# Modulation rows split over two stages: shift and scale by column quarters on turned tokens, gates and second norm during the first block's projections

## The chip, the cores and the metric

The kernel runs on one core of a Trainium2 chip. Its engines run in parallel and meet through semaphores: TensorE (PE, matrix products and transposes into PSUM; its weight loads are listed as PEld), VectorE (DVE), ScalarE (ACT), GpSimd (POOL) and SyncE (SP, which here only starts transfers). The metric is the time of one execution on the device in microseconds (us), smaller is better. The inputs are laid out on the host; all arithmetic is on the chip.

## What is computed

Two blocks of a transformer-like network over 1024 tokens of width 1024, all in 32-bit floats. What matters here is how the first block starts and where the vector `mod` goes:

```python
cond = jax.nn.silu(c)                              # (1, 1024)
mod = cond @ ada_w[l] + ada_b[l]                   # (1, 6144)
sh_m, sc_m, gt_m, sh_f, sc_f, gt_f = [t[:, None, :] for t in jnp.split(mod, N_MOD, axis=-1)]
h = rms_norm(x, norm_mix_g[l]) * (1.0 + sc_m) + sh_m
proj = jnp.einsum('bsd,de->bse', h, w_in[l])
...
x = x + gt_m * (merged @ w_out[l])
h = rms_norm(x, norm_mlp_g[l]) * (1.0 + sc_f) + sh_f
x = x + gt_f * (jnp.square(jax.nn.relu(h @ mlp_w1[l])) @ mlp_w2[l])
```

Only the first third of `mod` (sh_m, sc_m) is needed for the first projections. The other four vectors are needed when the mixers have been merged, far later.

## The kernel before

The program is a row of stages. Each is a `Stage`: it owns buffers and semaphores, and at its end all engines meet at a barrier, so no stage starts before the last instruction and the last awaited store of the one before. The stages that matter are "mod" (`mod_norm_stage`), then "scans", "diff_gemm" (`diff_gemm_stage`), "diff", and all the others behind them. Within a stage the order of each engine is the order in which it is written; there is no scheduler.

**The stage "mod".** SP loads the tokens `x` (8 tiles of 128 tokens, 4 MB) and then, through a ring of four 2 MB slots, the weights `ada_w` in 12 chunks of 512 columns (`NCH` is 12); a slot is loaded again when DVE has released it. ScalarE makes silu of the condition (`cact`, the 1024 values as 8 columns of 128) and the sums of squares of the token tiles (L216). For each chunk c:

- TensorE multiplies the first four of the eight k blocks of the chunk (L278): the stationary matrix is `cwide`, the condition repeated over 128 columns, so that the result stands on all 128 partitions;
- DVE does the other four k blocks as multiply-adds over 128x512 into `acc` (L231, `partial`), and TensorE sums `acc` over the partitions with a matrix of ones into the same PSUM bank (L280);
- DVE copies the chunk to `mod` (L240, `take`).

When chunks 0 to 3 (shift and scale) are there, DVE scales the gain once (L263), and then normalizes the token tiles, two passes each (`norm`: L245 and L246), two buffers `h` in turn. The table `NORMED` puts them behind chunks 4 to 9. TensorE turns each tile (8 transposes, L286, which in the program stand behind the products of the next chunk), and ScalarE moves it into `hT`, the turned tokens that all projections read (L221). POOL stores the rows of the chunks 4 to 11 (gates and second norm) to the array `mod_rows` in HBM (L204), and the stage waits for these stores. "scans" starts with its own loads (L2797) and splits `hT` and weights into high and low parts for three-pass products (L155, L156, L157).

**The stage "diff_gemm"** makes 24 result tiles n of 128x512, each by 8 k blocks of three passes on TensorE (L155 to L157), evicted by ScalarE (L1871) and stored by SP. Its weights come in five pieces (1 MB each from the second on), cast on ScalarE (L1862, L1866), and DVE subtracts to get the low part (`low_w`: L1881, L1885). TensorE waits for a piece at the tiles 8, 12, 16 and 20 (`LAST`). DVE has nothing else to do there, and POOL nothing at all. Its columns 0 to 511 of `oN` are not in use.

**Elsewhere**: the routers of the expert stages (L3430) already make products of 32 columns of weights at four column places of the array; they serve the prediction as a measure.

Of the kernel before, what the change touches and what calls it, by code (L numbers as in the profile page):

```python
# [6 lines left out]
F32 = mybir.dt.float32  # L7
# [6 lines left out]
P = 128  # L14
S = 1024
D = 1024
# [143 lines left out]
def mod_norm_stage(nc, m):  # L160


    with Stage(nc, "mod") as st:
        NCH, K2 = 6 * D // HALF, KD // 2
        first = m["ring"].take(NCH)
        x = m["oN"]
        ccol, cact = st.sb("ccol", [P, KD]), st.sb("cact", [P, KD])
        cwide, ones = st.sb("cwide", [P, K2, P]), st.sb("ones", [P, P])
        bias, mod = st.sb("bias", [P, NCH, HALF]), st.sb("mod", [P, NCH, HALF])
        acc = st.sb("acc", [P, 2, HALF])  # L170
        h, g = st.sb("h", [P, 2, D]), st.sb("gain", [P, D])
        ss, rs = st.sb("ss", [P, NT]), st.sb("rs", [P, NT])
        out, TP = st.ps("out", [P, 2, HALF]), st.ps("tp", [P, 2, KD, P])
        (loaded, zeroed, bias_in, act_done, wide, summed_up, summed, added, stored, squared, mean_in, root, gain_ready,
         scaled, h_ready, turned_up, tp_free, stepped) = (
            st.sem(x_) for x_ in ("loaded", "zeroed", "bias_in", "act_done", "wide", "summed_up", "summed", "added",
                                  "stored", "squared", "mean_in", "root", "gain_ready", "scaled", "h_ready", "turned_up",
                                  "tp_free", "stepped"))
        x_in = [st.sem(f"x_in{t}") for t in range(NT)]
        block = st.block()  # L180
        NORMED = {4: (0,), 5: (1, 2), 6: (3,), 7: (4, 5), 8: (6,), 9: (7,)}
        flat = mod[:, :, :].rearrange("p c n -> p (c n)")
        shift, scale = flat[:, 0:D], flat[:, D:2 * D]

        def slot(c):
            return m["ring"].slot(first + c, KD, HALF)

# [7 lines left out]
        def _(pool):  # L195
# [5 lines left out]
            pool.dma_start(bias[0:1, :, :].rearrange("p c n -> p (c n)"), m["ada_b"][0:1, :]).then_inc(bias_in, 16)  # L201
            for c in range(4, NCH, 2):
                pool.wait_ge(added, c + 2)
                pool.dma_start(m["mod"][0:1, c * HALF:(c + 2) * HALF], flat[0:1, c * HALF:(c + 2) * HALF])\  # L204
                    .then_inc(stored, 16)
            pool.wait_ge(stored, 16 * (NCH - 4) // 2)

        @block.scalar
        def _(act):
# [3699 lines left out]
```

## Time and profile before

| what | value |
|---|---|
| median of 3 runs | 4243.39 us (4241.23 to 4247.34) |
| the profiled execution, its own time | 4248.85 us |
| its span, first to last instruction | 4247.0 us |
| TensorE busy in the span | 3730.8 us (88%) |
| VectorE, ScalarE, GpSimd busy | 2463.2 (58%), 1626.5 (38%), 354.2 us (8%) |
| granted TensorE clock, mean | 0.939 of full |
| first transfer of the stage "scans" | at 104.27 us |
| "diff_gemm" | from 772.25 to 913.14 us |

The span starts with the first instruction. Because the stages meet at barriers, what a stage takes is the distance between the first transfers of two neighbours, and what one stage gets shorter, all later ones start earlier.

### The profile page before, as it was taken

What the parts mean: (1) busy time and instruction counts of PE and PEld (TensorE: products, weight loads), DVE (VectorE), ACT (ScalarE), POOL (GpSimd) and SP (SyncE); (2) the same over time, 40 slices, a digit from 0 to 9 for tenths busy, and PEclk for the clock granted to TensorE, in tenths of its full rate; (3) what the DMA queues carried; (4) which work ended last, traced back from release to release, by engine and by line L of the source; (5) the groups of instructions that cost most, each with busy time, mean ns of one, the idle gap of its engine ahead of it and who ended that gap; (6) DMA issues with size and microseconds to landing.
All of it is one profiled execution on the core that took longest, in us unless ns stands there. A gap on an engine that the chain in (4) does not pass through costs nothing. (4 is left out here: it accounts for less than half of the span.)

```text
span 4247.0 us, 58233 instructions
## 1 busy us (share of the span) xinstructions
PE 3730.8 (88%) x23192; PEld 3037.4 (72%) x23192; DVE 2463.2 (58%) x3913; ACT 1626.5 (38%) x2293; POOL 354.2 (8%) x205
## 2 busy tenths in 40 slices
PE   6988999989898999999798998499886998984996
PEld 2666778767777888888598776377686776773774
DVE  6257764129765655656332663777664666636785
ACT  2223342138531000002212763366534666623765
POOL 0001112000000000000000000144100000000441
PEclk9989999989999999999899999699898999996998
DMA  7201122331342111112222415399724103042997
GB/s 284 73 25 50 55 70 86 103 129 40 129 155 80 40 59 40 59 40 80 78 75 70 132 44 189 134 371 368 248 77 131 36 7 127 24 144 100 372 368 273
DMA packets 192273, 527.06 MB, mean 124 GB/s; under 512 B 27137, under 2 KB 126241, under 8 KB 174001
## 3 DMA queue, kind: packets, MB, share of 16 engines
q1 hardware_dynamic: 172576, 463.01, 30.0%
q0 software_dynamic: 16352, 58.84, 4.6%
q8 instruction: 156, 2.56, 0.2%
q10 hardware_dynamic: 3120, 2.10, 0.2%
q14 instruction: 69, 0.56, 0.0%
HBM read 432.52 MB, written 91.37 MB: 123 GB/s over the span
## 5 line engine op out<-in xcount | busy, mean ns | idle before, releaser
L2462 ACT ACTIVATE mlp_relu<-mlp_z 128x512 f32<-128x512 f32 x64 | 38.3, 598 | 616.0 <-PE mlp_z L157 616.0
L155 PE MATMUL scans_G<-ring_r 128*128 128x512 f32 x544 | 221.7, 408 | 32.3 <-ACT scans_stg L3009 18.3
L3584 DVE TENSOR_TENSOR ring_r<-ring,oN_r 128x4096 fp32r<-128x4096 f32 x48 | 212.4, 4426 | 64.1 <-ACT oN_r L3512 63.5
L3584 DVE TENSOR_TENSOR ring_r<-ring,hT_r 128x4096 fp32r<-128x4096 f32 x48 | 212.3, 4423 | 61.5 <-ACT hT_r L3512 61.4
L3512 ACT ACTIVATE oN_r<-ring 128x4096 fp32r<-128x4096 f32 x48 | 174.0, 3630 | 82.6 <-DMA ring<-in_w_all 68.4
L155 PE MATMUL mlp_z<-oN_r,mlp_w_high_r 128*128 128x512 f32 x512 | 200.2, 391 | 5.6 <-DVE ring_r L2503 5.6
L3512 ACT ACTIVATE hT_r<-ring 128x4096 fp32r<-128x4096 f32 x48 | 174.0, 3629 | 76.5 <-DMA ring<-in_w_all 76.5
L156 PE MATMUL mlp_z<-hT_r,mlp_w_high_r 128*128 128x512 f32 x512 | 199.9, 390 | 0.0
L157 PE MATMUL mlp_z<-oN_r,ring_r 128*128 128x512 f32 x512 | 199.9, 390 | 0.0
L155 PE MATMUL mlp_y_ps<-mlp_w_high_r,ring_r 128*128 128x512 f32 x512 | 199.6, 390 | 0.0
L157 PE MATMUL mlp_y_ps<-mlp_w_high_r,ring_r 128*128 128x512 f32 x512 | 199.2, 389 | 0.0
L156 PE MATMUL mlp_y_ps<-ring_r 128*128 128x512 f32 x512 | 199.2, 389 | 0.0
L3398 POOL TENSOR_TENSOR moe_taker<-moe_zero 128x1 f32<-128x1 f32 x63 | 160.5, 2548 | 412.1 <-ACT moe_y L3574 399.5
L156 PE MATMUL scans_G<-hT_r,ring_r 128*128 128x512 f32 x480 | 191.9, 400 | 0.0
L157 PE MATMUL scans_G<-ring_r 128*128 128x512 f32 x480 | 191.2, 398 | 0.0
L2513 DVE TENSOR_TENSOR mlp_relu<-mlp_relu 128x512 f32<-128x512 f32 x64 | 44.2, 691 | 182.0 <-ACT mlp_relu L2462 173.1
L155 PEld LDWEIGHTS scans_G<-ring_r 128*128 128x128 f32 x544 | 104.9, 193 | 59.1 <-issue 14.7
L2524 DVE TENSOR_TENSOR mlp_y<-mlp_y_ps,mlp_gt 128x512 f32<-128x512 f32 x128 | 88.2, 689 | 99.0 <-PE mlp_y_ps L157 96.6
L155 PE MATMUL even_gemm_acc<-even_gemm_w_high,ring_r 128*128 128x384 f32 x384 | 133.7, 348 | 5.0 <-DVE ring_r L673 5.0
L157 PE MATMUL even_gemm_acc<-even_gemm_w_high,hT_r 128*128 128x384 f32 x384 | 129.7, 338 | 0.0
L2860 POOL TENSOR_TENSOR ring_r<-ring,ring_r 128x2048 fp32r<-128x2048 f32 (+1 forms) x16 | 73.7, 4607 | 567.8 <-ACT ring_r L3014 567.8
L155 PEld LDWEIGHTS mlp_z<-oN_r,mlp_w_high_r 128*128 128x128 f32 x512 | 96.6, 189 | 26.1 <-issue 6.0
(666 smaller groups left out, 10196.4 us busy)
## 6 DMA issues: line engine op xcount, KB each, us to landing
ring<-in_w_all SPq DMA_DIRECT2D x118, 2048.0 KB, 10.7
ring<-in_w_mlp SPq DMA_DIRECT2D x16, 2048.0 KB, 8.4
ring<-in_w_all SPq DMA_DIRECT2D x12, 1024.0 KB, 6.2
branch_gates<-scans_stg SPq DMA_DIRECT2D x48, 256.0 KB, 2.0
merge_raw<-branch_gates SPq DMA_DIRECT2D x16, 768.0 KB, 5.1
ring<-in_w_even SPq DMA_DIRECT2D x4, 1536.0 KB, 6.7
qk_turned<-even_gemm_y SPq DMA_DIRECT2D x48, 128.0 KB, 1.9
ring<-qk_turned SPq DMA_DIRECT2D x6, 1024.0 KB, 5.0
```

Source lines behind the costliest of these rows:

```text
L155: pe.matmul(out, lh, rh, start=start, stop=False)
L156: pe.matmul(out, lh, rl, start=False, stop=False)
L157: return pe.matmul(out, ll, rh, start=False, stop=stop)
L2462: act.activation(r[:, n % 2, :], Z[:, n % 4, :], ACT.Relu).then_inc(z_free, 1)
L2513: step(dve.tensor_tensor(r[:, n % 2, :], r[:, n % 2, :], r[:, n % 2, :], ALU.mult))
L2524: dve.tensor_tensor(y[:, n % 2, :], Y[:, n % 4, :], gt[:, cols], ALU.mult).then_inc(y_free, 1)
L2860: pool.tensor_tensor(low, raw, high.bitcast(F32), ALU.subtract).then_inc(w_split, 1)
L3398: pool.tensor_tensor(taker[:, n:n + 1], zero[:], zero[:], ALU.add)
L3512: act.activation(w_high[n % RING], buf[:, (first + n) % RING, :], ACT.Copy).then_inc(w_cast, 1)
L3584: dve.tensor_tensor(buf_r[:, b, :], buf[:, b, :], w_high[n % RING].bitcast(F32), ALU.subtract)\
```

## The change

- "mod" takes only the chunks 0 to 3. The ring's limit goes from 12 to 4, the later `skip` from 8 to 16.
- For a chunk, TensorE now does all eight k blocks, as products with 32 columns of weights (`ccols`), k block k at the column quarter k % 4 of the array, so on 32 partitions each (`Q`). DVE adds the bias (`quart`), and one product with `sel` (ones at the partitions 0, 32, 64 and 96) sums the quarters on all partitions. `partial` is gone.
- The tokens are only scaled by their inverse root before they are turned, on ScalarE (`h`, in turn with the move into `hT`). Shift and (1 + scale) * gain are turned to columns (8 transposes each, into `Q` and `out`), and applied at the end to the eight 128x1024 blocks of `hT`: three on ScalarE, five on DVE.
- "diff_gemm" gets the chunks 4 to 11: POOL fills `SUMS` (in `oN`) with zeros and the bias, and loads 16 halves of chunks, 1 MB each, into three places (second halves of weight slots); DVE adds each with four multiply-adds of 128x512 behind each `low_w` (`add_part`). Ahead of tile 21, TensorE sums them over the partitions (8 products with 32 columns of ones), ScalarE moves the sums, and POOL stores the rows in `mod_rows`.

```diff
@@ -161,29 +161,32 @@
...
     with Stage(nc, "mod") as st:
-        NCH, K2 = 6 * D // HALF, KD // 2
+        NCH = 2 * D // HALF
...
-        ccol, cact = st.sb("ccol", [P, KD]), st.sb("cact", [P, KD])
-        cwide, ones = st.sb("cwide", [P, K2, P]), st.sb("ones", [P, P])
+        ccol, cact = st.sb("ccol", [P, KD]), m["cact"]
+        ccols, sel = st.sb("ccols", [P, KD, 32]), st.sb("sel", [P, P])
...
-        acc = st.sb("acc", [P, 2, HALF])
+        quart = st.sb("quart", [P, 2, HALF])
...
+        cols = st.sb("cols", [P, 2, KD])
+        Q, out, TP = st.ps("quarters", [P, 2, HALF]), st.ps("out", [P, 2, HALF]), st.ps("tp", [P, 2, KD, P])
...
-        NORMED = {4: (0,), 5: (1, 2), 6: (3,), 7: (4, 5), 8: (6,), 9: (7,)}
...
+        ON_ACT = (5, 6, 7)
...
-            pool.dma_start(bias[0:1, :, :].rearrange("p c n -> p (c n)"), m["ada_b"][0:1, :]).then_inc(bias_in, 16)
-            for c in range(4, NCH, 2):
-                pool.wait_ge(added, c + 2)
-                pool.dma_start(m["mod"][0:1, c * HALF:(c + 2) * HALF], flat[0:1, c * HALF:(c + 2) * HALF])\
-                    .then_inc(stored, 16)
-            pool.wait_ge(stored, 16 * (NCH - 4) // 2)
+            pool.dma_start(bias[0:1, :, :].rearrange("p c n -> p (c n)"), m["ada_b"][0:1, 0:2 * D]).then_inc(bias_in, 16)
+            pool.memset(sel[:], 0.0).then_inc(zeroed, 1)
+            pool.wait_ge(zeroed, 2)
+            for j in range(4):
+                pool.memset(sel[32 * j:32 * j + 1, :], 1.0).then_inc(sel_in, 1)
...
@@ -216,75 +218,100 @@
                 act.activation(h[:, 0, :], x[:, t, :], ACT.Square, accum_out=ss[:, t:t + 1]).then_inc(squared, 1)
             act.wait_ge(mean_in, 1)
             act.activation(rs[:], ss[:], ACT.Sqrt).then_inc(root, 1)
-            for t in range(NT):
-                act.wait_ge(turned_up, t + 1)
-                act.activation(m["hT"][:, :, t * P:(t + 1) * P], TP[:, t % 2, :, :], ACT.Copy).then_inc(tp_free, 1)
+            act.wait_ge(squared, NT)
+            act.wait_ge(inverse, 1)
+            for t in range(NT + 1):
+                if t < NT:
+                    if t >= 2:
+                        act.wait_ge(turned_up, t - 1)
+                    act.activation(h[:, t % 2, :], x[:, t, :], ACT.Copy, scale=rs[:, t:t + 1]).then_inc(h_ready, 1)
+                if t >= 1:
+                    act.wait_ge(turned_up, t)
+                    act.activation(m["hT"][:, :, (t - 1) * P:t * P], TP[:, (t - 1) % 2, :, :], ACT.Copy).then_inc(tp_free, 1)
+            act.wait_ge(tp_free, NT)
+            act.wait_ge(cols_in, 1)
+            for k in ON_ACT:
+                act.activation(m["hT"][:, k, :], m["hT"][:, k, :], ACT.Identity, bias=cols[:, 1, k:k + 1],
+                               scale=cols[:, 0, k:k + 1])
...
         @block.vector
...
-            def partial(c):
-                w, a = slot(c), acc[:, c % 2, :]
-                m["ring"].wait(dve, first + c)
-                for k in range(K2, KD):
-                    ins = dve.scalar_tensor_tensor(a, w[:, k, :], cact[:, k:k + 1], bias[:, c, :] if k == K2 else a,
-                                                   ALU.mult, ALU.add)
-                    if k < KD - 1:
-                        step(ins)
-                ins.then_inc(summed_up, 1)
...
             def take(c):
                 dve.wait_ge(summed, c + 1)
-                m["ring"].release(dve)
-                dve.tensor_copy(mod[:, c, :], out[:, c % 2, :]).then_inc(added, 1)
-
-            def norm(t):
-                if t >= 2:
-                    dve.wait_ge(turned_up, t - 1)
-                step(dve.scalar_tensor_tensor(h[:, t % 2, :], x[:, t, :], rs[:, t:t + 1], g[:], ALU.mult, ALU.mult))
-                dve.tensor_tensor(h[:, t % 2, :], h[:, t % 2, :], shift, ALU.add).then_inc(h_ready, 1)
+                if c < NCH // 2:
+                    dve.tensor_copy(mod[:, c, :], out[:, c % 2, :]).then_inc(taken, 1)
+                else:
+                    n = (c - NCH // 2) * HALF
+                    dve.scalar_tensor_tensor(mod[:, c, :], out[:, c % 2, :], 1.0, g[:, n:n + HALF], ALU.add, ALU.mult)\
+                       .then_inc(taken, 1)
...
             dve.wait_ge(act_done, 1)
-            step(dve.memset(ones[:], 1.0))
-            dve.tensor_copy(cwide[:], cact[:, 0:K2].unsqueeze(2).to_broadcast([P, K2, P])).then_inc(wide, 1)
+            dve.tensor_copy(ccols[:, :, :], cact[:].unsqueeze(2).to_broadcast([P, KD, 32])).then_inc(wide, 1)
...
             for c in range(NCH):
-                partial(c)
+                dve.wait_ge(waved, c + 1)
+                m["ring"].release(dve)
+                if c >= 2:
+                    dve.wait_ge(summed, c - 1)
+                dve.tensor_tensor(quart[:, c % 2, :], Q[:, c % 2, :], bias[:, c, :], ALU.add).then_inc(quartered, 1)
                 if c >= 1:
                     take(c - 1)
-                if c == 3:
-                    dve.wait_ge(squared, NT)
-                    dve.tensor_scalar(ss[:], ss[:], 1.0 / D, EPS, ALU.mult, ALU.add).then_inc(mean_in, 1)
-                    dve.wait_ge(root, 1)
-                    step(dve.reciprocal(rs[:], rs[:]))
-                if c == 4:
-                    dve.wait_ge(added, 4)
-                    step(dve.scalar_tensor_tensor(g[:], scale, 1.0, g[:], ALU.add, ALU.mult))
-                for t in NORMED.get(c, ()):
-                    norm(t)
             take(NCH - 1)
+            dve.wait_ge(shift_turned, 1)
+            dve.tensor_copy(cols[:, 1, :].unsqueeze(2), blocks(Q)[:, :, 0:1])
+            dve.wait_ge(gain_turned, 1)
+            dve.tensor_copy(cols[:, 0, :].unsqueeze(2), blocks(out)[:, :, 0:1]).then_inc(cols_in, 1)
+            dve.wait_ge(cols_in, 1)
+            dve.wait_ge(tp_free, NT)
+            for k in range(KD):
+                if k not in ON_ACT:
+                    dve.tensor_scalar(m["hT"][:, k, :], m["hT"][:, k, :], cols[:, 0, k:k + 1], cols[:, 1, k:k + 1],
+                                      ALU.mult, ALU.add)
...
         @block.tensor
         def _(pe):
+            def turn(t):
+                pe.wait_ge(h_ready, t + 1)
+                if t >= 2:
+                    pe.wait_ge(tp_free, t - 1)
+                for k in range(KD):
+                    ins = pe.transpose(TP[:, t % 2, k, :], h[:, t % 2, k * P:(k + 1) * P], m["ident"][:])
+                ins.then_inc(turned_up, 1)
...
             pe.wait_ge(wide, 1)
             pe.wait_ge(m["ident_in"], 16)
+            pe.wait_ge(sel_in, 4)
             for c in range(NCH):
                 w = slot(c)
                 m["ring"].wait(pe, first + c)
                 if c >= 2:
-                    pe.wait_ge(added, c - 1)
-                for k in range(K2):
-                    pe.matmul(out[:, c % 2, :], cwide[:, k, :], w[:, k, :], start=k == 0, stop=False)
-                pe.wait_ge(summed_up, c + 1)
-                pe.matmul(out[:, c % 2, :], ones[:], acc[:, c % 2, :], start=False, stop=True).then_inc(summed, 1)
...
+                    pe.wait_ge(quartered, c - 1)
+                for k in range(KD):
+                    j = slice(32 * (k % 4), 32 * (k % 4) + 32)
+                    ins = pe.matmul(Q[j, c % 2, :], ccols[:, k, :], w[:, k, :], start=k < 4, stop=k >= 4)
+                ins.then_inc(waved, 1)
+                turn(2 * c)
+                if c + 1 < NCH:
+                    turn(2 * c + 1)
+                pe.wait_ge(quartered, c + 1)
+                if c >= 2:
+                    pe.wait_ge(taken, c - 1)
+                pe.matmul(out[:, c % 2, :], sel[:], quart[:, c % 2, :], start=True, stop=True).then_inc(summed, 1)
+            pe.wait_ge(taken, 2)
+            for k in range(KD):
+                ins = pe.transpose(blocks(Q)[:, k, :], flat[:, k * P:(k + 1) * P], m["ident"][:])
+            ins.then_inc(shift_turned, 1)
+            turn(NT - 1)
+            pe.wait_ge(taken, NCH)
+            for k in range(KD):
+                ins = pe.transpose(blocks(out)[:, k, :], flat[:, D + k * P:D + (k + 1) * P], m["ident"][:])
+            ins.then_inc(gain_turned, 1)
...
@@ -1789,7 +1816,16 @@
...
+        rows = st.ps("rows", [P, 2, HALF])
...
+        PARTS, SUMS = 16, m["oN"][:, :, 0:HALF]
+        parts = [t_[:, b, SLOT // 2:SLOT].rearrange("p (k n) -> p k n", n=HALF) for t_, b in ((buf, 1), (more, 0), (more, 1))]
@@ -1831,9 +1867,35 @@
...
+        @block.gpsimd
+        def _(pool):
+            pool.memset(ONE[:], 1.0).then_inc(ones_in, 1)
+            pool.memset(SUMS, 0.0).then_inc(zeroed, 1)
+            pool.wait_ge(zeroed, 1)
+            pool.dma_start(SUMS[0:1, :, :], m["ada_b"][0:1, 2 * D:6 * D].rearrange("o (c n) -> o c n", n=HALF))\
+                .then_inc(bias_in, 16)
+            for i in range(PARTS):
+                if i >= len(parts):
+                    pool.wait_ge(part_added, i - len(parts) + 1)
+                c, half = divmod(i, 2)
+                pool.dma_start(parts[i % len(parts)], m["w_all"][4 + c, :, half * SLOT // 2:(half + 1) * SLOT // 2]
+                               .rearrange("p (k n) -> p k n", n=HALF)).then_inc(part_in[i % len(parts)], 16)
+            pool.wait_ge(rows_out, 2)
+            for c in range(PARTS // 2):
+                pool.dma_start(m["mod"][0:1, 2 * D + c * HALF:2 * D + (c + 1) * HALF],
+                               parts[0][32 * (c % 4):32 * (c % 4) + 1, c // 4, :]).then_inc(rows_stored, 16)
+            pool.wait_ge(rows_stored, 16 * PARTS // 2)
...
         @block.tensor
         def _(pe):
             for n in range(N):
+                if n == N - 3:
+                    pe.wait_ge(ones_in, 1)
+                    pe.wait_ge(sums_done, 1)
+                    for c in range(PARTS // 2):
+                        ins = pe.matmul(rows[32 * (c % 4):32 * (c % 4) + 32, c // 4, :], ONE[:], SUMS[:, c, :],
+                                        start=True, stop=True)
+                    ins.then_inc(rows_done, 1)
@@ -1869,6 +1931,10 @@
...
                 act.activation(x[:, n % KEEP, :], A[:, n % 4, :], ACT.Copy).then_inc(x_in, 1)
+                if n == N - 3:
+                    act.wait_ge(rows_done, 1)
+                    for j in range(2):
+                        act.activation(parts[0][:, j, :], rows[:, j, :], ACT.Copy).then_inc(rows_out, 1)
...
+            def add_part(i):
+                c, half = divmod(i, 2)
+                dve.wait_ge(part_in[i % len(parts)], 16 * (i // len(parts) + 1))
+                for k in range(4):
+                    kk = 4 * half + k
+                    ins = dve.scalar_tensor_tensor(SUMS[:, c, :], parts[i % len(parts)][:, k, :], m["cact"][:, kk:kk + 1],
+                                                   SUMS[:, c, :], ALU.mult, ALU.add)
+                    if k < 3:
+                        step(ins)
+                ins.then_inc(part_added, 1)
+                dve.wait_ge(part_added, i + 1)
+
+            step = Steps(dve, stepped)
+            dve.wait_ge(bias_in, 16)
             for s_ in range(1, NS):
                 low_w(s_)
+                for i in range(4 * s_ - 4, 4 * s_):
+                    add_part(i)
+            dve.nop().then_inc(sums_done, 1)
@@ -3709,12 +3792,13 @@
...
-        m["ring"].limit = 12
...
+        m["ring"].limit = 4
...
-        m["ring"].skip(8)
+        m["ring"].skip(16)
```

How TensorE's order changes in the stage "mod". Before, from the end of chunk 4 on (`mod_tp` are the turned tokens; the pattern goes on to chunk 11):

```order
L280 MATMUL mod_out<-mod_acc,mod_ones 128x512
L278 MATMUL mod_out<-ring,mod_cwide 128x512 x4
L280 MATMUL mod_out<-mod_acc,mod_ones 128x512
L286 MATMUL mod_tp<-identity,mod_h 128x128 x8
L278 MATMUL mod_out<-ring,mod_cwide 128x512 x4
L280 MATMUL mod_out<-mod_acc,mod_ones 128x512
L286 MATMUL mod_tp<-identity,mod_h 128x128 x16
L278 MATMUL mod_out<-ring,mod_cwide 128x512 x4
L280 MATMUL mod_out<-mod_acc,mod_ones 128x512
```

The same engine and stage now, the last two chunks and the end of the stage:

```order
L297 MATMUL mod_quarters<-ring,mod_ccols 32x512 x8
L284 MATMUL mod_tp<-identity,mod_h 128x128 x16
L305 MATMUL mod_out<-mod_quart,mod_sel 128x512
L297 MATMUL mod_quarters<-ring,mod_ccols 32x512 x8
L284 MATMUL mod_tp<-identity,mod_h 128x128 x8
L305 MATMUL mod_out<-mod_quart,mod_sel 128x512
L308 MATMUL mod_quarters<-identity,mod_mod 128x128 x8
L284 MATMUL mod_tp<-identity,mod_h 128x128 x8
L313 MATMUL mod_out<-identity,mod_mod 128x128 x8
```

The tiles are now turned from the first chunk on, and nothing of chunks 4 to 11 is left. DVE in "diff_gemm", from its second piece of weights on, now (before, these splits, then L1881, followed each other with nothing between):

```order
L1947 TENSOR_TENSOR ring_r<-ring,diff_gemm_w_high 128x2048
L1958 SCALAR_TENSOR_TENSOR oN<-ring,cact,oN 128x512 x4
L1958 SCALAR_TENSOR_TENSOR oN<-diff_gemm_more,cact,oN 128x512 x8
L1958 SCALAR_TENSOR_TENSOR oN<-ring,cact,oN 128x512 x4
L1947 TENSOR_TENSOR diff_gemm_more_r<-diff_gemm_more,diff_gemm_w_high 128x2048
L1958 SCALAR_TENSOR_TENSOR oN<-diff_gemm_more,cact,oN 128x512 x8
L1958 SCALAR_TENSOR_TENSOR oN<-ring,cact,oN 128x512 x4
L1958 SCALAR_TENSOR_TENSOR oN<-diff_gemm_more,cact,oN 128x512 x4
L1947 TENSOR_TENSOR diff_gemm_more_r<-diff_gemm_more,diff_gemm_w_high 128x2048
```

So 16 multiply-adds stand behind each split of weights, 64 in all, and the last split has 16 multiply-adds of the third group ahead of it.

## Rows read from the trace of the kernel before

**Rows 1.** Busy time of each engine in the two changed stages.
```profile
core 0: us, PE busy (x) PEld busy (x) DVE busy (x) ACT busy (x) POOL busy (x), PEclk, DMA share, GB/s
0.00:104.27 104.27, 66.22 (x184) 31.81 (x184) 64.48 (x81) 20.15 (x28) 9.75 (x13) 0.96 0.71 288
772.25:913.14 140.89, 132.99 (x576) 109.57 (x576) 13.66 (x6) 25.28 (x30) 0.00 (x0) 0.97 0.22 75
```

**Rows 2.** Groups by line up to 105 us: mean ns, then idle time before.
```profile
L278 PE MATMUL mod_out<-ring,mod_cwide 128*128 128x512 f32 x96 | 45.8, 622 | 22.1 <-DMA ring<-in_w_all 22.1
L231 DVE SCALAR_TENSOR_TENSOR mod_acc<-ring,mod_cact,mod_acc 128x512 f32<-128x512 f32 x36 | 27.1, 752 | 1.3
L221 ACT ACTIVATE hT<-mod_tp 128x1024 f32<-128x1024 f32 x8 | 8.1, 1023 | 48.0 <-PE mod_tp L286 48.0
```

**Rows 3.** Timeline of the end of the stage "mod", and first transfer of "scans".
```profile
99.97 0.69 DVE L240 COPY mod_mod<-mod_out 128x512 f32<-128x512 f32 x1 [2.28 <-PE mod_out L280]
100.96 0.48 POOL L204 DMA_DIRECT2D mod_rows<-mod_mod  x1 [6.11 <-DVE mod_mod L240]
104.27 0.40 SPq L2797 DMA_DIRECT2D scans_c<-in_w_all  x1
```

**Rows 4.** Timeline: ScalarE's table load; DVE at the first and fourth slot.
```profile
20.20 1.28 ACT L218 ACT_TABLE_LOAD   x1
21.85 0.75 DVE L231 SCALAR_TENSOR_TENSOR mod_acc<-ring,mod_cact,mod_bias 128x512 f32<-128x512 f32 x1 [10.68 <-DMA ring<-in_w_all]
36.45 0.75 DVE L231 SCALAR_TENSOR_TENSOR mod_acc<-ring,mod_cact,mod_bias 128x512 f32<-128x512 f32 x1 [1.18 <-DMA ring<-in_w_all]
```

**Rows 5.** Timeline of TensorE in "mod"; each product is two passes (x8 are four).
```profile
21.88 6.09 PE L278 MATMUL mod_out<-ring,mod_cwide 128*128 128x512 f32 x8 [21.88 <-DMA ring<-in_w_all]
28.67 3.60 PE L278 MATMUL mod_out<-ring,mod_cwide 128*128 128x512 f32 x8
53.01 1.04 PE L286 MATMUL mod_tp<-identity,mod_h 128*128 128x128 f32 x8
60.58 1.80 PE L280 MATMUL mod_out<-mod_acc,mod_ones 128*128 128x512 f32 x2 [3.10 <-DVE mod_acc L231]
```

**Rows 6.** Timeline of weight loads at the routers of the two expert stages.
```profile
2647.61 0.20 PEld L3430 LDWEIGHTS moe_u_ps<-hT,moe_wr_wide 128*32 128x32 f32 x4 [0.66 <-issue]
2648.46 0.20 PEld L3430 LDWEIGHTS moe_u_ps<-hT,moe_wr_wide 128*32 128x32 f32 x4 [0.66 <-issue]
...
3829.54 0.12 PEld L3430 LDWEIGHTS moe_u_ps<-hT,moe_wr_wide 128*32 128x32 f32 x4 [0.34 <-issue]
3829.97 0.12 PEld L3430 LDWEIGHTS moe_u_ps<-hT,moe_wr_wide 128*32 128x32 f32 x4 [0.31 <-issue]
```

**Rows 7.** Groups by form: 128x1024 in SBUF with a scalar for each partition.
```profile
L3194 DVE TENSOR_SCALAR scans_T<-scans_T,scans_om 128x1024 f32<-128x1024 f32 x4 | 3.0, 751 | 0.1
L3077 ACT ACTIVATE scans_KQ<-scans_KQ,scans_lb 128x1024 f32<-128x1024 f32 x4 | 4.4, 1141 | 0.0
```

**Rows 8.** Timeline of DVE in "diff_gemm", second and last piece of weights.
```profile
792.35 2.29 DVE L1881 TENSOR_TENSOR ring_r<-ring,diff_gemm_w_high 128x2048 fp32r<-128x2048 f32 x1 [13.64 <-ACT diff_gemm_w_high L1862]
868.51 2.29 DVE L1881 TENSOR_TENSOR ring_r<-ring,diff_gemm_w_high 128x2048 fp32r<-128x2048 f32 x1 [19.47 <-ACT diff_gemm_w_high L1862]
```

**Rows 9.** Timeline of ScalarE and SP: the tiles 20 and 23, the next stage.
```profile
893.27 0.60 ACT L1871 ACTIVATE diff_gemm_x<-diff_gemm_acc 128x512 f32<-128x512 f32 x1 [4.84 <-PE diff_gemm_acc L157]
909.59 0.60 ACT L1871 ACTIVATE diff_gemm_x<-diff_gemm_acc 128x512 f32<-128x512 f32 x1 [4.84 <-PE diff_gemm_acc L157]
913.14 0.34 SPq L1934 DMA_DIRECT2D diff_lp<-in_diff_lambda  x1
```

**Rows 10.** Issues of transfers: KB each, us from issue to landing.
```profile
diff_gemm_more<-in_w_diff SPq DMA_DIRECT2D x2, 1024.0 KB, 9.7
x_rows<-out_x POOLq DMA_DIRECT2D x8, 512.0 KB, 2.9
qk_turned<-diff_gemm_x SPq DMA_DIRECT2D x16, 256.0 KB, 2.0
mod_rows<-mod_mod POOLq DMA_DIRECT2D x4, 4.0 KB, 3.7
```

More of the change, by code:

```diff
@@ L171, in mod_norm_stage @@
         h, g = st.sb("h", [P, 2, D]), st.sb("gain", [P, D])
         ss, rs = st.sb("ss", [P, NT]), st.sb("rs", [P, NT])
[L173 to L178, printed above, removed]
+        cols = st.sb("cols", [P, 2, KD])
@@ new lines, in mod_norm_stage @@
+        Q, out, TP = st.ps("quarters", [P, 2, HALF]), st.ps("out", [P, 2, HALF]), st.ps("tp", [P, 2, KD, P])
+        (loaded, zeroed, sel_in, bias_in, act_done, wide, waved, quartered, summed, taken, squared, mean_in, root, inverse,
+         h_ready, turned_up, tp_free, shift_turned, gain_turned, cols_in, stepped) = (
+            st.sem(x_) for x_ in ("loaded", "zeroed", "sel_in", "bias_in", "act_done", "wide", "waved", "quartered", "summed",
+                                  "taken", "squared", "mean_in", "root", "inverse", "h_ready", "turned_up", "tp_free",
+                                  "shift_turned", "gain_turned", "cols_in", "stepped"))
@@ L179, in mod_norm_stage, with blocks @@
         x_in = [st.sem(f"x_in{t}") for t in range(NT)]
         block = st.block()
-        NORMED = {4: (0,), 5: (1, 2), 6: (3,), 7: (4, 5), 8: (6,), 9: (7,)}
         flat = mod[:, :, :].rearrange("p c n -> p (c n)")
-        shift, scale = flat[:, 0:D], flat[:, D:2 * D]
+        ON_ACT = (5, 6, 7)
         def slot(c):
             return m["ring"].slot(first + c, KD, HALF)
+        def blocks(ps):
+            return ps[:, :, :].rearrange("p a n -> p (a n)").rearrange("p (k n) -> p k n", n=P)
@@ L251, in _ @@
+            dve.wait_ge(act_done, 1)
+            dve.tensor_copy(ccols[:, :, :], cact[:].unsqueeze(2).to_broadcast([P, KD, 32])).then_inc(wide, 1)
+            dve.wait_ge(squared, NT)
+            dve.tensor_scalar(ss[:], ss[:], 1.0 / D, EPS, ALU.mult, ALU.add).then_inc(mean_in, 1)
+            dve.wait_ge(root, 1)
+            dve.reciprocal(rs[:], rs[:]).then_inc(inverse, 1)
             dve.wait_ge(bias_in, 16)
             for c in range(NCH):
-                partial(c)
+                dve.wait_ge(waved, c + 1)
[3 more added lines that the diff above has]
+                dve.tensor_tensor(quart[:, c % 2, :], Q[:, c % 2, :], bias[:, c, :], ALU.add).then_inc(quartered, 1)
@@ L275, in _ @@
                 if c >= 2:
-                    pe.wait_ge(added, c - 1)
-                for k in range(K2):
-                    pe.matmul(out[:, c % 2, :], cwide[:, k, :], w[:, k, :], start=k == 0, stop=False)
-                pe.wait_ge(summed_up, c + 1)
-                pe.matmul(out[:, c % 2, :], ones[:], acc[:, c % 2, :], start=False, stop=True).then_inc(summed, 1)
-                for t in NORMED.get(c - 1, ()):
-                    pe.wait_ge(h_ready, t + 1)
-                    if t >= 2:
-                        pe.wait_ge(tp_free, t - 1)
-                    for k in range(KD):
-                        ins = pe.transpose(TP[:, t % 2, k, :], h[:, t % 2, k * P:(k + 1) * P], m["ident"][:])
-                    ins.then_inc(turned_up, 1)
+                    pe.wait_ge(quartered, c - 1)
[19 more added lines that the diff above has]
+            ins.then_inc(gain_turned, 1)
 def norm_stage(nc, m, name, src, gain, out=None):
@@ L1791, in diff_gemm_stage @@
         A = st.ps("acc", [P, 4, HALF])
+        ONE = st.sb("ones", [P, 32])
+        rows = st.ps("rows", [P, 2, HALF])
         w_cast, w_split, done, x_in = (st.sem(s_) for s_ in ("w_cast", "w_split", "done", "x_in"))
+        stepped = st.sem("stepped")
+        (zeroed, ones_in, bias_in, part_added, sums_done, rows_done, rows_out, rows_stored) = (
+            st.sem(s_) for s_ in ("zeroed", "ones_in", "bias_in", "part_added", "sums_done", "rows_done", "rows_out",
+                                  "rows_stored"))
+        PARTS, SUMS = 16, m["oN"][:, :, 0:HALF]
+        parts = [t_[:, b, SLOT // 2:SLOT].rearrange("p (k n) -> p k n", n=HALF) for t_, b in ((buf, 1), (more, 0), (more, 1))]
+        part_in = [st.sem(f"part_in{b}") for b in range(len(parts))]
         w_in = [st.sem(f"w_in{b}") for b in range(RING)]
@@ L3711, in build_program @@
         m["up_in"] = [ctx.enter_context(nc.semaphore(f"up_in{j}")) for j in range(2)]
-        m["ring"].limit = 12
+        m["cact"] = ctx.enter_context(nc.sbuf_tensor("cact", [P, KD], F32))
+        m["ring"].limit = 4
         mod_norm_stage(nc, m)
         scans_stage(nc, m)
-        m["ring"].skip(8)
+        m["ring"].skip(16)
         m["ring"].limit = BEFORE_MLP
```

## The prediction

> **What bounds the kernel now.** I first split the span by stage. The stages meet at barriers, so the question is what the first 104.27 us and the 140.89 us of "diff_gemm" are made of [rows 1]. In "mod" neither PE (66.2 us busy) nor DVE (64.5 us) is full: the reader should see two engines at some 60% that take turns. The groups by line then say what fills them [rows 2]: 36 + 12 multiply-adds of 0.75 us on DVE for half of each weight chunk, 96 passes on PE for the other half. Slots of weights arrive every 4.9 us (slot 0 at 21.85, slot 3 at 36.45 [rows 4]); twelve would be in by about 21.9 + 11 x 4.9 = 76 us, so at the end the stage is not bound by loads but by the exchange between DVE and PE. Last come a copy that ends at 100.66, a store issued at 100.96, and the barrier, 3.3 us behind it [rows 3].
>
> In "diff_gemm" PE is busy for 133 of 140.9 us [rows 1], and DVE for 13.7. The tile evictions end at 910.2; the next stage starts at 913.14, after a store of 2.0 us and a barrier of about 1 us [rows 9, 10]. Anything that PE gets to do there costs its full time; what DVE gets costs nothing, up to a point.
>
> **The stage "mod" after, step by step.** Its start doesn't change: the same bytes stand ahead of the first four slots, so slot 0 is in at 21.9 and slot 3 at 36.45 [rows 4]. ScalarE's eight squares are done when it loads the table for the root, until 21.5 [rows 4]; with root and inverse (about 0.6) and a scaled copy (1.1 [rows 7]) the first tile is ready near 23.3, while PE is still at the first chunk. From 21.9 on I count PE's work, since with only four chunks everything hangs on its written order.
>
> - Chunk products. Eight products in 32 columns are 16 passes. At the routers, four weight loads, so four passes, went out every 0.85 us at the low and every 0.43 us at the high level of the clock [rows 6]: the four column places run side by side. That a full-width pass takes the same 0.43 us shows in 3.60 us for eight [rows 5]. So a chunk costs 4 x 0.43 = 1.7 us. The first comes at the low level: eight passes took 6.09 us from 21.88 on, as against 3.60 us later [rows 5], so it takes 3.4 us. Sum 3.4 + 3 x 1.7 = 8.5 us.
> - Eight turned tiles at 1.04 us [rows 5], the first about 1 us more at the low level: 9.3 us.
> - Four products with `sel`, two passes each, 0.9 us: 3.6 us.
> - Shift and gain to columns: 2 x 1.04 = 2.1 us.
> - Waits of PE. ScalarE alternates a scaled copy (up to 1.14 us [rows 7]) and a move into `hT` (1.02 us [rows 2]), so 2.2 us a tile or 4.3 us for two; PE needs 1.7 + 2.1 + 0.9 = 4.7 us for a chunk with its two tiles. They are nearly equal, and PE is a little slower; I allow 1 us. Slot 3 is in before PE asks for it. DVE's bias add (0.7 us, as the copy of the same shape [rows 3]) lies beside the turned tiles.
>
> So PE ends at 21.9 + 8.5 + 9.3 + 3.6 + 2.1 + 1.0 = 46.4. Then come two tiny copies and their semaphores (0.4), and the pass over `hT`: DVE 5 x 0.75 = 3.75, ScalarE 3 x 1.14 = 3.4 us side by side [rows 7]. That gives 50.5; no store is waited for, so only the 1 us of the barrier follows, and "scans" starts at about 51.5 instead of 104.27: **52.8 us less**. The bounds: if PE never waits and the copies are free, 50; if PE waits at each of four chunks for 1 us and the first five us of low clock become eight, 56. "scans" itself is the same program, with the same idle PE ahead of it, so it moves as a whole.
>
> **The stage "diff_gemm" after.** What it adds:
>
> - PE: 8 products with 32 columns of ones at four column places ahead of tile 21, 16 passes, 1.7 us by [rows 6]; this is on the path. Were they one after the other, 16 x 0.43 = 6.9 us. I take **1.7 us**.
> - DVE: 64 multiply-adds. 36 of them took 27.1 us, 0.75 each [rows 2], and about 0.78 with the semaphore between dependent ones; a part is 3.1 us, 16 parts 50 us. The second piece of weights is split until 794.6, the last until 870.8 [rows 8]; each time 12.5 us of parts follow, in gaps of 20 to 30 us. So parts 12 to 15 end near 883.5, and PE asks for the sums ahead of tile 21, when tile 20 is done at 893.2 [rows 9]. Cover of about 10 us.
> - POOL: zeros into 128x4096, then loads of 1 MB. Three are in flight; a new one starts when the oldest place is added. With 0.5 us to issue, up to 9.7 us to land (the slowest of this size, three together [rows 10]) and 3.1 us of adding, a place turns over in 13.3 us, so a part comes at least every 4.4 us; the last group then ends at 870.8 + 17.8 = 888.6, still ahead of 893.2. For the optimistic end, POOL's own stores of half the size landed in 2.9 us while DVE worked [rows 10]. What is behind the waiting DVE is the next split of weights; that of the last piece is asked for 20 us after it is made. No charge.
> - The tail. ScalarE moves the sums behind tile 21 (near 901 + 1.2), POOL issues 8 stores of 0.49 us, and the last lands 3.7 us later [rows 3, 10]: about 910, while the stage ends at 912 + 1.7. No charge, but only 4 us of cover.
>
> On POOL's loads a rule speaks against the change. The Trainium skill, "SBUF — State Buffer", section "Who interferes with whom", says that a transfer started from GpSimd can't get its descriptors written while DVE runs an operation in a mode that uses both of its port pairs. The rows of this trace say that the multiply-add isn't in the faster mode: it takes 0.752 us for 512 elements [rows 2], where a tensor-scalar takes 0.751 us for 1024 [rows 7]. By the rule the loads then stay free; no run of before has DVE's multiply-adds beside POOL's loads, so it stays a rival below.
>
> **Sum.** -52.8 + 1.7 = -51.1 us. Against the profiled execution's own 4248.85 this is 4197.7; that one lies 5.5 us above the median, and against the median of 4243.39 the forecast is **4192 us** (-1.2%). A change within 0.2%, 8.5 us, is what a measurement here can't tell from none.
>
> **Rivals.**
>
> - *PE stays slow in "mod"*, or the column places don't run side by side there. An idle time of 3.1 us was followed by two passes in 1.80 us instead of 0.9 [rows 5], so gaps bring the low level back. For it: ScalarE and PE are closely matched, so small gaps come each tile. Against: I find none above 1 us. Price: the 20.8 us of work at the high level doubled, less what I had, +18 us or so: 4210. Chance 7%.
> - *Loads of the parts are late.* PE waits at tile 21 when a part takes more than (893.2 - 870.8) / 4 = 5.6 us. With p us each, back to back from 794.6, and 6.9 us for three splits, the wait is 794.6 + 16p + 6.9 - 893.2 = 16p - 91.7. At p = 7 this is 20 us: 4212. Chance 8%.
> - *The other side: slower.* If POOL's descriptors only get through when DVE stands still, loading and adding take turns: 3.1 + 0.5 + 6 us for a load alone (1 MB; between 2.9 for half and 9.7 with company [rows 10]), p = 9.6, a wait of 62 us, which takes back the 51: 4254. It decides from p = (91.7 + 51.1) / 16 = 8.9 us on. The evidence on the multiply-add's speed is against it. Chance 3%, and 2% for a p that ends within 0.2% of before.
> - *The change doesn't do what it says*: "mod" bound by loads anyway. The fourth slot is in at 36.45 [rows 4], so this can't hold it beyond my 46.4, and it is in the sum.
>
> **How the numbers follow.** The forecast has 80%, with a range of its own of 4187 to 4199 (stage end 50 to 56, PE's extra 1.7 to 6.9, some 3 us for what medians of three runs scatter). The two cases of late loads and slow PE, 15%, lie around 4205 to 4215; the upper end takes in their smaller half, so that some 12% with the slower cases are left out above and a few below. Range 4185 to 4207. Faster 95%, same 2%, slower 3%.
>
> **What the profile after would show.** First transfer of "scans" near 51.5; chunk products of 16 passes in 1.7 us, 3.4 the first; PE's last transposes ending near 46; five tensor-scalars of 0.75 us; no POOL store ahead of the barrier. In "diff_gemm", 16 groups of multiply-adds in four clusters, each done 8 us or more ahead of the next split, the last near 883 - 53 = 830; no wait at the row products, and 142.6 us from its first transfer to that of the next stage. Wrong would be: PE waiting for DVE ahead of tile 21, the stage ended by POOL's stores, or "mod" ending later than 57, with gaps on PE ahead of turned tiles.

## The result and the profile after

The changed kernel took 4221.53 us (median of 5 runs, 4215.26 to 4222.4), the one before 4243.39 in the runs beside it: the ratio is 0.994, with a 95% interval of 0.9929 to 0.9951. It is faster, by 22 us, where 51 were forecast. The profiled execution took 4215.72 us of its own time (span 4214.0); the working of the prediction had 4197.7 for it, so 18.0 us are missing there. (Between the medians 29 are missing. Single executions scatter: the profiled one of before lies 5.5 us above its median, that of after 5.8 below. The accounts by stage below go by the profiled ones.)

The first question is in which stage they are missing. The first transfers of neighbouring stages give the length of each. These are the rows of SP's timeline of the kernel after, at the starts of "scans", "diff_gemm", "diff", "mlp" and "spatial":

```profile
48.80 0.38 SPq L2880 DMA_DIRECT2D scans_c<-in_w_all  x1
716.12 0.56 SPq L1851 DMA_DIRECT2D ring<-in_w_diff  x1
862.19 0.34 SPq L2017 DMA_DIRECT2D diff_lp<-in_diff_lambda  x1
1262.66 0.38 SPq L2461 DMA_DIRECT2D mlp_x<-x_rows  x1
2004.92 0.33 SPq L2686 DMA_DIRECT2D spatial_gn<-in_even_gmlp_norm  x1
```

And the last two of them in the kernel before:

```profile
1310.12 0.38 SPq L2378 DMA_DIRECT2D mlp_x<-x_rows  x1
2034.37 0.33 SPq L2603 DMA_DIRECT2D spatial_gn<-in_even_gmlp_norm  x1
```

| stretch | before | after | difference | forecast |
|---|---|---|---|---|
| "mod" | 104.27 | 48.80 | -55.5 | -52.8 |
| "scans" | 667.98 | 667.32 | -0.7 | 0 |
| "diff_gemm" | 140.89 | 146.07 | +5.2 | +1.7 |
| from "diff" up to "mlp" | 396.98 | 400.47 | +3.5 | 0 |
| "mlp" | 724.25 | 742.26 | +18.0 | 0 |
| behind "mlp" | 2212.6 | 2209.1 | -3.5 | 0 |

The part that was worked out came out better than forecast. The missing time lies in "mlp", a stage that the diff doesn't touch. What is different there shows in a window of 200 us in its middle, where TensorE is busy all the time in both kernels, so that only the number of passes can differ (columns as in [rows 1]). Before:

```profile
1600.00:1800.00 200.00, 200.00 (x884) 165.62 (x883) 115.51 (x139) 11.97 (x20) 0.00 (x0) 1.00 0.14 52
```

After:

```profile
1600.00:1800.00 200.00, 200.00 (x861) 161.47 (x860) 116.42 (x138) 9.59 (x16) 0.00 (x0) 1.00 0.11 42
```

884 passes have become 861: one takes 232.3 ns where it took 226.2. The granted clock is 1.00 in both; DVE's busy time differs by 0.9 us of 200, ScalarE does less, and the transfers are no denser. The stage has 3072 such passes (six groups of 512), and 6.0 ns on each are 18.5 us, about the 18.0 that the stage got longer. Over the whole stage PE's busy time went from 709.3 to 727.6 us, 18.3 more. The groups by line say the same. Three of the six in the page of before:

```profile
L155 PE MATMUL mlp_z<-oN_r,mlp_w_high_r 128*128 128x512 f32 x512 | 200.2, 391 | 5.6 <-DVE ring_r L2503 5.6
L155 PE MATMUL mlp_y_ps<-mlp_w_high_r,ring_r 128*128 128x512 f32 x512 | 199.6, 390 | 0.0
L156 PE MATMUL mlp_y_ps<-ring_r 128*128 128x512 f32 x512 | 199.2, 389 | 0.0
```

And in that of after:

```profile
L155 PE MATMUL mlp_z<-oN_r,mlp_w_high_r 128*128 128x512 f32 x512 | 203.0, 396 | 5.6 <-DVE ring_r L2586 5.6
L155 PE MATMUL mlp_y_ps<-mlp_w_high_r,ring_r 128*128 128x512 f32 x512 | 204.1, 399 | 0.0
L156 PE MATMUL mlp_y_ps<-ring_r 128*128 128x512 f32 x512 | 201.4, 393 | 0.0
```

(A row's mean is the length of one pass, some 0.39 us; the next one starts 0.23 us after it, so passes overlap.) Idle time ahead of the first is 5.6 us, as before: it isn't a wait. The passes themselves are longer.

### The profile page after: what moved, and what is told of

The parts are those of the page before. It is cut to its first block and busy times, and to the rows that moved or that the text cites. A ratio compares the mean times of both kernels' runs of the same rounds, so it can differ in the third digit from the quotient of the medians.

```text
span 4214.0 us, 58214 instructions
## 1 busy us (share of the span) xinstructions
PE 3713.1 (88%) x23176; PEld 3016.2 (72%) x23176; DVE 2456.5 (58%) x3914; ACT 1639.8 (39%) x2306; POOL 366.4 (9%) x233
## 5 line engine op out<-in xcount | busy, mean ns | idle before, releaser
L155 PE MATMUL scans_G<-ring_r 128*128 128x512 f32 x544 | 222.1, 408 | 32.3 <-ACT scans_stg L3092 18.3
L156 PE MATMUL mlp_z<-hT_r,mlp_w_high_r 128*128 128x512 f32 x512 | 202.3, 395 | 0.0
L156 PE MATMUL mlp_y_ps<-ring_r 128*128 128x512 f32 x512 | 201.4, 393 | 0.0
L156 PE MATMUL scans_G<-hT_r,ring_r 128*128 128x512 f32 x480 | 191.5, 399 | 0.0
```

The source lines that it names most:

```text
L155: pe.matmul(out, lh, rh, start=start, stop=False)
L156: pe.matmul(out, lh, rl, start=False, stop=False)
```

## The experiments

**What could reach a stage that isn't touched.** Three things differ there: its addresses in SBUF, what "diff_gemm" leaves behind (a queue of GpSimd in use), and what the engine and its clock did up to that point. In the diff one line bears on the addresses of all stages: `m["cact"] = ctx.enter_context(nc.sbuf_tensor("cact", [P, KD], F32))`, in `build_program` ahead of all the stages' own buffers. Its 32 bytes in a partition move each of them. These are the start addresses in the built programs, in bytes in a partition:

```
                  ring    hT     oN      diff_gemm_w_high  mlp_w_high
before            16512   82048  114816  180864            193152
after             16512   82048  114816  180896            193184
```

So my theory A: passes are slower when the buffers that they read lie at another distance from each other in SBUF. B: the work put into "diff_gemm" leaves something behind. C: the shorter first stage puts later ones into another phase of the clock or of the loads.

**pad32: before, with 32 unused bytes there.** Nothing else of the change is in it.

```diff
+        m["pad"] = ctx.enter_context(nc.sbuf_tensor("pad", [P, 8], F32))
         m["ring"].limit = 12
```

> The kernel before with nothing changed but an unused buffer of 32 bytes a partition, allocated where the change puts cact, so that the buffers of all stages lie 32 bytes further on, as in the changed kernel. Theory A (the displaced buffers make TensorE's 512-column passes take 231 to 233 ns instead of 227): slower than before by 19 to 26 us, with passes of 231 to 233 ns in the stage mlp. Theory B (something that the new work in diff_gemm leaves behind, its loads from POOL or DVE's work): no change. Theory C (the shorter first stage changes the clock): no change.

Measured: 4272.78 us, ratio 1.0063 (1.0049 to 1.0076), slower by some 30 us. The window in "mlp", as above:

```profile
1600.00:1800.00 200.00, 200.00 (x862) 161.43 (x861) 106.10 (x132) 11.39 (x19) 0.00 (x0) 1.00 0.11 42
```

SP's rows give 742.3 us for "mlp" (1314.62 to 2056.92) and 143.9 for "diff_gemm" (771.48 to 915.39). A buffer that no instruction uses costs what was missing, a little more than the 19 to 26 us expected, with neither the first stage nor the work in "diff_gemm" changed. That carries A, and neither B nor C is needed.

**cact64: after, with 64 bytes for the buffer instead of 32.**

```diff
-        m["cact"] = ctx.enter_context(nc.sbuf_tensor("cact", [P, KD], F32))
+        m["cact"] = ctx.enter_context(nc.sbuf_tensor("cact", [P, 2 * KD], F32))[:, 0:KD]
```

> The changed kernel with cact given 64 bytes a partition instead of 32, of which the second half is unused, and nothing else. Theory A: passes back at 227 ns in diff_gemm and mlp, and the time that was predicted from the stages, about 4190 us, some 50 to 54 below before. Theories B and C: as the changed kernel, about 4215 to 4222.

Measured: 4225.08 us, 0.9953 (0.994 to 0.9967), and 862 passes in the window. 64 bytes are no better than 32: what theory A was expected to give here, some 4190 us, didn't come, so 64 isn't the unit.

**dgonly: before's "mod" with after's "diff_gemm"** and `m["cact"]` at 64 bytes; the ring's limit stays 12, the later `skip` 8.

> The stage mod of the kernel before, with all twelve chunks, and the added work of the change in diff_gemm (loads by POOL, 64 multiply-adds, row sums, stores, which write the same rows a second time), with cact at 64 bytes. Theory A: slower than before by what TensorE's row sums cost, 1.7 to 3 us, passes at 227 ns. Theory B: slower by 19 us or more, passes of 231 to 233 ns from diff_gemm on. Theory C: 1.7 to 3 us.

Measured: 4277.1 us, 1.0081 (1.0067 to 1.0094), 863 passes. That is 35 us where A was expected to give 1.7 to 3, because 64 bytes were taken for harmless. By itself it can't tell B from A, since the buffer is in it; dg512 below does.

**mlp32: before, with 32 bytes as the first buffer of "mlp" alone.**

```diff
+        pad = st.sb("pad", [P, 8])
```

> The kernel before with an unused buffer of 32 bytes a partition at the start of the stage mlp alone. Theory A, in its local form: slower than before by about 14 to 17 us (some 3100 passes of 512 columns, 5 ns each), all of it in mlp, stages behind it unchanged. If the displacement acts otherwise than on the stage's own operands: no change here. Theories B and C: no change.

Measured: 4262.19 us, 1.0045 (1.0031 to 1.0058); 862 passes in "mlp", while "diff_gemm" kept its length (769.38 to 910.22, 140.8 us). "mlp" itself took 741.0 us, 16.7 more than before (1308.50 to 2049.47), and the stretch behind it 1.7 less. The cost is local: the stage whose buffers are moved pays.

**cact128: 128 bytes** (`[P, 4 * KD]`, same line as in cact64).

> The changed kernel with cact given 128 bytes a partition, of which the first 32 are used, so that every stage's buffers start at the same address modulo 128 as in the kernel before. If the displacement modulo 128 is the whole loss (theory A as the first four runs left it: 32 and 64 bytes both cost): passes of 226.7 ns in diff_gemm and mlp, 51 us or a little more below before, 4188 to 4194. If any displacement costs, or the change has a cost of its own beside it: 4210 to 4230.

**all128: cact128, and every buffer of every stage filled up to a multiple of 128 bytes.**

```diff
+        got = self.ctx.enter_context(self.nc.sbuf_tensor(f"{self.name}_{name}", shape, dt))
+        size = int(np.prod(shape[1:])) * (1 if dt == U8 else 4)
+        rest = -(-(-size // 32) * 32) % 128
+        if rest:
+            self.ctx.enter_context(self.nc.sbuf_tensor(f"{self.name}_{name}_fill", [P, rest // 4], F32))
+        return got
```

> As cact128, and every buffer of a stage is followed by unused bytes up to a multiple of 128, so that also those of the expert stages, at 32 modulo 128 in all kernels so far, start at a multiple of 128. Theory A: passes in the expert stages go from 233 to 227 ns; if TensorE sets the pace there, another 15 to 20 us less than cact128, if the loads do (DMA share 0.98 to 1.00 there), no more than 5. A theory in which these stages are slow for the transfers beside them: passes stay at 233.

Measured: 4212.86 (0.9922, 0.9908 to 0.9936) and 4213.11 us (0.9922, 0.9908 to 0.9937). Both have the same row of passes but for the small engines; cact128:

```profile
1600.00:1800.00 200.00, 200.00 (x868) 162.59 (x867) 116.17 (x138) 9.60 (x16) 0.00 (x0) 1.00 0.12 43
```

128 bytes give back 7 of 23 passes, so 128 is not the unit. all128 adds one thing: in the first expert stage, where a pass took some 233 ns from its start to the next one's in before and in cact128, it took 228, and the time of the kernel stayed as it was. The transfers' share from 2700 to 2900 us is 0.99 and 0.98 in the two: the stage is bound by its loads, so shorter passes buy nothing. The groups of the same products from 2700 to 2900 us, cact128 and then all128:

```profile
L156 PE MATMUL moe_g_ps<-ring_r,moe_x_high 128*128 128x512 f32 x84 | 33.2, 395 | 0.0
```

```profile
L161 PE MATMUL moe_g_ps<-ring_r,moe_x_high 128*128 128x512 f32 x83 | 32.3, 390 | 0.0
```

**mlpw32: before, with 32 bytes in "mlp" right ahead of `w_high`**, so that `x` and what stands ahead of the weights keep their places. **mlpx32: 32 bytes first, and 96 ahead of `w_high`**, so that `x` moves by 32 and `w_high` by 128.

```diff
+        pad = st.sb("pad", [P, 8])
...
+        pad2 = st.sb("pad2", [P, 24])
```

> The kernel before with 32 unused bytes in the stage mlp right ahead of w_high, the only buffer of the stage's own that TensorE's passes read; the tokens, sums and relu buffers stay. If TensorE's reading of a displaced operand is what costs: all of the 20 us that the displacement of the whole stage cost. If it is the other engines' or the transfers' buffers: no change.

> The counterpart: in the stage mlp the buffers of tokens, gate, sums and relu are displaced by 32 bytes, and 96 more unused bytes put w_high back at a multiple of 128. If TensorE's reading of a displaced operand is what costs: no change. If it is the others': slower by up to 20 us.

Measured: mlpw32 4261.7 us (1.0034, 1.002 to 1.0047) with 862 passes, the whole loss of mlp32 within the error; mlpx32 4258.2 us (1.003, 1.0019 to 1.0041) with 867. The first says that the place of `w_high` and of what stands behind it is enough. The expectation of no change for the second was wrong: it took 128 bytes for a distance that costs nothing, and 867 is what cact128 shows for 128 (868). So mlpx32 tells nothing of `x`; it repeats cact128 in one stage.

**cact256 and cact512: after, with 256 and 512 bytes** (`8 * KD`, `16 * KD`).

> The changed kernel with cact at 256 bytes a partition. In the kernel before, ring, hT, oN and all weight buffers of the stages up to the experts start at 128 modulo 512; displacements of the stages' buffers by 32, 64 and 128 bytes against ring, hT and oN all cost. If the distance of the two counts modulo 256: passes of 226.7 ns in mlp and about 4190 us. If modulo 512 only: some 4210 to 4225, as with 128.

> The changed kernel with cact at 512 bytes a partition, so that all distances modulo 512 are those of the kernel before. If the distance is the loss (theory A in this form): passes of 226.7 ns in diff_gemm and mlp, and 51 us below before, 4188 to 4195. If not, as with 128: about 4213.

Measured: cact256 4188.6 us (4185.45 to 4197.79), 0.9861 (0.9846 to 0.9877); cact512 4194.63 us (4192.98 to 4198.59), 0.988 (0.9865 to 0.9895). The windows, cact256 first:

```profile
1600.00:1800.00 200.00, 200.00 (x884) 165.59 (x883) 108.65 (x135) 11.37 (x19) 0.00 (x0) 1.00 0.14 52
```

```profile
1600.00:1800.00 200.00, 200.00 (x884) 165.68 (x883) 108.98 (x137) 11.37 (x19) 0.00 (x0) 1.00 0.14 52
```

All 884 passes are back, with the shorter first stage in place, so C falls. The starts of "mlp" and "spatial" in cact512 are 724.31 us apart, as before (724.25):

```profile
1254.60 0.38 SPq L2461 DMA_DIRECT2D mlp_x<-x_rows  x1
1978.91 0.33 SPq L2686 DMA_DIRECT2D spatial_gn<-in_even_gmlp_norm  x1
```

**dg512: dgonly with 512 bytes instead of 64.** The same work in "diff_gemm", the distance restored.

> The stage mod of the kernel before with the added work in diff_gemm (as dgonly), with cact at 512 bytes a partition. Theory A: slower than before by the row sums of TensorE alone, 1.7 to 3 us, instead of 35. If the added work itself costs: 20 us or more.

Measured: 4247.77 us, 1.0002 (0.9993 to 1.0011), 884 passes. B falls: the moved work leaves nothing behind that costs time. The rows of SP at the two ends of "diff_gemm":

```profile
770.84 0.55 SPq L1824 DMA_DIRECT2D ring<-in_w_diff  x1
913.92 0.34 SPq L1990 DMA_DIRECT2D diff_lp<-in_diff_lambda  x1
```

These are 143.1 us, 2.2 more than before, which is what the eight row products cost when the buffers lie as before.

**first32: before, with 32 bytes ahead of the ring**, so that ring, `hT`, `oN` and all stages' buffers move together.

```diff
+        m["pad"] = ctx.enter_context(nc.sbuf_tensor("pad", [P, 8], F32))
         m["ring"] = Ring(nc, ctx, m["w_all"])
```

> The kernel before with 32 unused bytes a partition ahead of the ring, so that all buffers, ring, hT and oN too, are displaced alike. If the distance between the stages' buffers and ring, hT and oN counts: no change. If the address of a buffer by itself counts: slower by 20 to 31 us.

Measured: 4245.9 us, 0.9999 (0.999 to 1.0008):

```profile
1600.00:1800.00 200.00, 200.00 (x884) 165.59 (x883) 115.70 (x138) 11.96 (x20) 0.00 (x0) 1.00 0.14 52
```

Here `mlp_w_high` stands at 193184, the same address as after the change, and the passes are at full pace. It isn't the address but the distance between the buffers. These are all the kernels, with the bytes by which `w_high` of "mlp" is displaced against ring, `hT` and `oN`:

| displaced by | kernels | passes in 200 us of "mlp" |
|---|---|---|
| 0 | before, first32 | 884 |
| 32 | after, pad32, mlp32, mlpw32 | 861, 862, 862, 862 |
| 64 | cact64, dgonly | 862, 863 |
| 128 | cact128, all128, mlpx32 | 868, 868, 867 |
| 256 | cact256 | 884 |
| 512 | cact512, dg512 | 884, 884 |

In before all distances between these buffers are multiples of 256 bytes (193152 - 82048 = 434 x 256).

One row limits what may be said of a single pass. Both operands of the group L156 `mlp_y_ps<-ring_r` lie in the ring, at the same distance in all kernels, and it still went from 389 to 393 ns in the pages above. Its passes stand between two that read `w_high`. So the cost isn't tied to the two operands of one pass; passes beside it take part. The three groups `scans_G` of "scans", whose passes follow one another and read ring and `hT` alone, are as they were: 408, 400 and 398 ns before, 408, 399 and 398 after.

## Why the prediction was right or wrong

**The step that failed** is the one on what lies behind the two stages: "'scans' itself is the same program, with the same idle PE ahead of it, so it moves as a whole", and then nothing for any later stage. For "scans" it held (-0.7 us). For the stages behind it it failed: they are the same instructions, but not at the same places. `m["cact"]` was given no cost; its 32 bytes displaced each stage's buffers against ring, `hT` and `oN`, and in "mlp" TensorE's passes went from 226 to 232 ns. That is +18.0 us in "mlp" and +3.0 in "diff_gemm" (146.07 against the 143.05 of cact512, where only the buffer's size differs). Part of the +3.5 between "diff" and "mlp" may be the same: this stretch takes 397.5 to 401.1 us in the kernels whose buffers are displaced there by 32 to 128 bytes, and 394.7 to 398.3 in the others, but the two ranges overlap and no run tests it alone. None of the prediction's rivals had displaced buffers. With that loss taken away the forecast's sum stands: cact512's profiled execution took 4194.36 us of its own time, against 4197.7 worked out, and by medians it is 50.6 us below before, against 51.1.

**"mod": right, 2.7 us better than said.** TensorE's timeline after (first chunk, first pair of tiles, second chunk, the last transposes, then the pass over `hT`):

```profile
21.80 3.58 PE L297 MATMUL mod_quarters<-ring,mod_ccols 128*32 128x512 f32 x16 [21.80 <-DMA ring<-in_w_all]
25.32 1.97 PE L284 MATMUL mod_tp<-identity,mod_h 128*128 128x128 f32 x16
28.08 1.92 PE L297 MATMUL mod_quarters<-ring,mod_ccols 128*32 128x512 f32 x16
42.86 1.04 PE L313 MATMUL mod_out<-identity,mod_mod 128*128 128x128 f32 x8
44.20 3.70 DVE L274 TENSOR_SCALAR hT<-hT,mod_cols 128x1024 f32<-128x1024 f32 x5
44.20 3.51 ACT L234 ACTIVATE hT<-hT,mod_cols 128x1024 f32<-128x1024 f32 x3
```

The first chunk took 3.58 us (3.4 forecast), the others 1.92 (1.7), and the four column places did run side by side. The 0.43 us for four passes side by side was a little low: 1.92 / 4 is 0.48, and the 3.60 us for eight that it was compared with are 0.45 each. The 1 us allowed for waits and the 1 us for a first tile at the low level weren't needed: the first two tiles took 1.97 us together, and from 21.80 to 43.90 PE's rows follow one another without a gap. So PE ended at 43.9 instead of 46.4, and the rest (0.3 for the copies, 3.7 for the pass, 0.9 for the barrier) was as said. The rival of a slow TensorE in "mod" didn't come. The six kernels with this "mod" end it between 47.4 and 49.0 us.

**"diff_gemm": cover and mechanism right, size off.** The timeline after, DVE's last split and parts, the row products, the stores:

```profile
814.33 2.29 DVE L1947 TENSOR_TENSOR ring_r<-ring,diff_gemm_w_high 128x2048 fp32r<-128x2048 f32 x1 [7.63 <-ACT diff_gemm_w_high L1924]
825.98 3.11 DVE L1958 SCALAR_TENSOR_TENSOR oN<-ring,cact,oN 128x512 f32<-128x512 f32 x4
839.68 1.92 PE L1896 MATMUL diff_gemm_rows<-oN,diff_gemm_ones 128*32 128x512 f32 x16
849.26 3.85 POOL L1885 DMA_DIRECT2D mod_rows<-ring  x8 [28.80 <-ACT ring L1937]
```

The last part ends at 829.1 (830 forecast), 10.6 us ahead of the row products, which wait for nothing. The parts ahead of the last split end 7.6 us before it (8 or more were said), so DVE's splits were never late. The row products take 1.92 us, and with the gap around them 2.2 (dg512), for 1.7 forecast. The last store is issued at 853.1 and a store of this kind lands in 1.7 us, so 7 us before the stage ends, not 4. Of the +5.2 us measured, 2.2 are the products and 3.0 the displaced buffers.

**Late loads and blocked descriptors: neither came.** In the groups and issues of the stage after:

```profile
L1958 DVE SCALAR_TENSOR_TENSOR oN<-diff_gemm_more,cact,oN 128x512 f32<-128x512 f32 x40 | 30.1, 752 | 1.3
L1881 POOL DMA_DIRECT2D diff_gemm_more<-in_w_all x10 | 5.3, 532 | 51.3 <-DVE oN L1958 51.3
```

```profile
ring<-in_w_all POOLq DMA_DIRECT2D x6, 1024.0 KB, 6.1
mod_rows<-ring POOLq DMA_DIRECT2D x8, 2.0 KB, 1.7
```

A multiply-add keeps its 752 ns beside GpSimd's loads [rows 2], an issue takes 0.53 us, a load of 1 MB lands 6.1 us later while DVE adds. Within a group parts follow each other every 3.15 us, so p, for which 5.6 was the point of waiting, was DVE's own adding. What the Trainium skill ("SBUF — State Buffer", "Who interferes with whom") says of GpSimd's descriptors is about DVE's modes that use both port pairs. At 752 ns for 512 elements, where a tensor-scalar does 1024 in 751 [rows 7], the multiply-add isn't in one, and the trace agrees with the rule: none of the 16 issues took longer than 0.57 us.

**What stays open.** The runs show that the distance counts and that 256 bytes more cost nothing; they don't show by what mechanism, nor which buffers must fit each other: `w_high` was moved against all three at once, and `x` alone was not tried. The times of the kernel after fall between 4215 and 4222, and those of cact256 between 4185 and 4198, without a row that says why; whether cact256 is truly ahead of cact512 is not settled by them. Both are faster than the kernel before and than the one after; the best that was measured is cact256, 4188.6 us.

## What to carry to other kernels

A new buffer is part of a change's cost even if it is tiny: before the later stages of a kernel are called unchanged, compare the addresses of their buffers. If a stage that the diff doesn't touch gets longer with TensorE busy throughout, count its passes in a window of fixed length; fewer passes at the same granted clock point at the places of the buffers that they read, and a pad of 32 bytes in the old kernel tests that in one run. Here new shared buffers should be rounded up to 256 bytes, which was worth 27 to 33 us in 4222 (cact512, cact256); where a stage waits for its loads, shorter passes were worth nothing (all128).

## What was unexpected of the hardware

- In "mlp" a 512-column pass takes 226 ns when the distances between the buffers that TensorE reads are multiples of 256 bytes, and 230 to 232 ns at 32, 64 or 128 bytes more (884 passes in 200 us against 868 and 861 to 863). Moving all buffers alike by 32 bytes changed nothing (first32). 32 unused bytes cost this kernel 0.63%.
- Passes that read none of the displaced buffers are slower too when their neighbours do (389 to 393 ns for L156 in the ring).
- It is not smooth: 32 and 64 bytes cost the same, 128 about a quarter to a third less, 256 and 512 nothing.
- Four products with 32 columns of weights each, at the four column places, ran side by side: 16 passes of 512 columns in 1.92 us, 0.48 us for four.
